# First block's attention: filler and output reads placed ahead of the row maxima, and the first query chunks rotated inside the third weight unit

## What is computed

```
for l in range(2):
    h = rmsnorm(x, g_pre_mix[l]);  z = h @ w_in[l]
    zf, zq, zk, zv, zm = split(z)            # Fourier, queries, keys, values, memory queries
    y_f = real(fft over tokens and channels of zf) @ w_f
    q, k = rope(zq), rope(zk)
    y_a = window attention(q, k, v)          # 8 query heads, 2 key heads, |i - j| <= 128, with a sink
    mkv = rmsnorm(mem) @ w_mem_kv[l]         # keys and values of 256 memory tokens
    y_m = memory attention(zm, mkv)          # 4 heads
    y = concat(rmsnorm of y_f, y_a, y_m) @ w_out[l]
    x = x + rmsnorm(y)
    x = x + rmsnorm(swiglu(rmsnorm(x)))
```

## Time and profile before

| | us |
|---|---|
| median of three runs | 3774.41 |
| lowest and highest | 3772.91 and 3779.49 |
| the profiled execution | 3766.36 |
| span of the core in that execution | 3764.6 |

### The profile page before, as it was taken

How to read it: one execution, slowest core, us unless ns; L and a number is a source line. 1 busy time by engine, 2 the same in 40 slices (tenths; PEclk the granted TensorE clock), 3 DMA queues, 4 the chain that set the end, 5 groups by cost and what they waited for, 6 DMA issues and landing times.

```text
span 3764.6 us, 49780 instructions
## 1 busy us (share of the span) xinstructions
PE 3558.8 (95%) x19681; PEld 2957.8 (79%) x19681; DVE 2481.9 (66%) x3545; ACT 1622.2 (43%) x2413; POOL 55.2 (1%) x82
## 2 busy tenths in 40 slices
PE   5899999889999999998899999999999989999999
PEld 4568997557998799886467889889988646778997
DVE  6548863656883688557665588649864766657862
ACT  3435542443553356325423345425542443234552
POOL 0000000000000000000000000000000000000000
PEclk8999999999999999999999999999999989999999
DMA  4212332212232233231123223223333211232332
GB/s 129 69 34 79 102 101 90 75 57 67 92 112 100 67 103 111 95 101 53 34 56 90 90 90 113 95 95 99 104 103 93 73 37 45 79 100 79 112 101 84
DMA packets 320877, 321.05 MB, mean 85 GB/s; under 512 B 11081, under 2 KB 292885, under 8 KB 320661
## 3 DMA queue, kind: packets, MB, share of 16 engines
q1 hardware_dynamic: 316308, 307.94, 25.9%
q0 software_dynamic: 2560, 8.26, 0.7%
q10 hardware_dynamic: 1792, 1.86, 0.2%
HBM read 315.92 MB, written 2.10 MB: 84 GB/s over the span
## 4 chain that ended last, share of the span: by engine, by line
PE 79%; DVE 15%; ACT 3%; issue 2%; DMA 0%; POOL 0%; ACTq 0%; DVEq 0%; POOLq 0%
PE products L733 31%; PE products L872 23%; PE products L770 6%; PE small L770 6%; PE small L872 4%; PE products L1066 2%; DVE conv L2588 2%; DVE w_lo L1877 1%; DVE seven_x L2110 1%; ACT w_hi L1330 1%; PE small L931 1%; DVE X L1892 1%; DVE x_sums L2099 1%; PE products L950 1%; PE products L1088 1%
## 5 line engine op out<-in xcount | busy, mean ns | idle before, releaser
L1877 DVE TENSOR_TENSOR w_lo<-raw,w_hi 128x2048 fp32r<-128x2048 f32 x190 | 435.3, 2291 | 528.8 <-ACT w_hi L1330 528.5
L1330 ACT ACTIVATE w_hi<-raw 128x2048 fp32r<-128x2048 f32 x190 | 363.4, 1913 | 943.6 <-PE products L733 691.8
L733 PE MATMUL products<-a_hi,w_hi 128*128 128x512 f32 (+1 forms) x1296 | 532.1, 411 | 35.4 <-DVE a_lo L1932 10.9
L733 PE MATMUL products<-a_lo,w_hi 128*128 128x512 f32 (+1 forms) x1296 | 519.7, 401 | 0.0
L733 PE MATMUL products<-a_hi,w_lo 128*128 128x512 f32 (+1 forms) x1296 | 519.5, 401 | 0.0
L872 PE MATMUL products<-seven_x,w_hi 128*128 128x256 f32 x2592 | 469.3, 281 | 7.7 <-DVE w_lo L2139 3.8
L872 PEld LDWEIGHTS products<-seven_x,w_hi 128*128 128x128 f32 x2592 | 398.0, 189 | 11.2 <-DVE w_lo L2139 5.1
L872 PE MATMUL products<-seven_x,more_hi 128*128 128x256 f32 x1632 | 381.7, 283 | 1.7 <-ACT rs_b L1421 1.7
L872 PE MATMUL products<-seven_x,w_lo 128*128 128x256 f32 x1296 | 363.1, 280 | 0.0
L733 PEld LDWEIGHTS products<-a_hi,w_hi 128*128 128x128 f32 (+1 forms) x1296 | 246.4, 190 | 109.4 <-issue 34.7
L733 PEld LDWEIGHTS products<-a_lo,w_hi 128*128 128x128 f32 (+1 forms) x1296 | 247.0, 191 | 63.7 <-issue 4.4
(11 more groups left out here) (421 smaller groups left out, 7372.4 us busy)
## 6 DMA issues: line engine op xcount, KB each, us to landing
raw<-in_ffn_w SPq DMA_DIRECT2D x244, 512.0 KB, 4.3
raw<-in_w_in SPq DMA_DIRECT2D x108, 512.0 KB, 4.8
raw<-in_w_ffn_in SPq DMA_DIRECT2D x88, 512.0 KB, 4.4
raw<-in_w_ffn_out SPq DMA_DIRECT2D x40, 512.0 KB, 4.4
raw<-in_w_out SPq DMA_DIRECT2D x32, 512.0 KB, 4.3
raw<-in_ffn_w SPq DMA_DIRECT2D x24, 384.0 KB, 3.5
raw<-in_w_mem_kv SPq DMA_DIRECT2D x8, 512.0 KB, 4.1
dft<-in_dft POOLq DMA_DIRECT2D x2, 2048.0 KB, 8.5
```

What stands on the lines that cost most here:

```text
L733: mm = pe.matmul(G[pair][0:m, into + b, 0:n], w[:, s, at:at + m], x, start=(first or into > 0) and k == 0 and q == 0, stop=(last or ends) ...
L1330: act.activation(w_hi[:, s, :], raw[:, s, :], ACT.Copy).then_inc(hi_ready, 1)
L1877: dve.tensor_tensor(w_lo[:, s, :], raw[:, s, :], w_hi[:, s, :].bitcast(F32), ALU.subtract).then_inc(lo_ready, 1)
```

## The change

Two orders are changed, both inside the first block's mixer.

First, query chunks 0 and 1 are rotated (`rotated_queries(0)`) at the end of the hook `during_queries`, into the pair `G` that the third unit does not use, and VectorE finishes them ahead of reading the third unit's result. `B4` and `B5` are no longer used for queries. Behind the third unit TensorE waits until its result is read, then rotates chunks 2 and 3 into the same spare pair. VectorE copies `B7` to `rs_b` ahead of making the low half of the fourth unit, and a new semaphore `spread_read` tells TensorE that `B7` is free.

Second, in the loop VectorE reads most fillers and all outputs of quad i-2 ahead of the maxima of quad i. Fillers 4 and 6 keep their place behind the maxima, since they are written in the same step.

```
                     mm.then_inc(four_ready, 1)
+                    rotated_queries(0)
+                spare = 1 - c.group % 2
+                def rotated_queries(first):
+                    pe.wait_ge(read_out[spare], c.next(f"read_out{spare}"))
+                    for i in range(2):
+                        pe.matmul(G[spare][:, i, :], c1["rot_q"][:], qT[:, first + i, :],
+                                  start=True, stop=True).then_inc(rot_ready, 1)
...
                 spread(MEM)
-                evicted((c.group - 2) % 2)
-                for i in range(2):
-                    pe.wait_ge(rot_used, c.next("rot_used"))
-                    pe.matmul((B4, B5)[i][:], c1["rot_q"][:], qT[:, i, :], start=True, stop=True).then_inc(rot_ready, 1)
-                pair = c.group % 2
-                pe.wait_ge(read_out[pair], c.next(f"read_out{pair}"))
-                evicted(1 - pair)
-                for i in range(2, 4):
-                    pe.matmul(G[pair][:, i - 2, :], c1["rot_q"][:], qT[:, i, :], start=True, stop=True).then_inc(rot_ready, 1)
+                evicted(1 - spare)
+                rotated_queries(2)
+                pe.wait_ge(four_copied, c.now("four_copied") + 1)
+                pe.wait_ge(spread_read, c.next("spread_read"))
+                pe.wait_ge(rot_used, c.next("rot_used", 2))
```

```
                 last.then_inc(diag_ready, 1)
+                late = 1 - c.group % 2
+                queries((G[late][:, 0, :], G[late][:, 1, :]), 0, late)
                 piece()
                 scaled(qT[:, 2:4, :], group(), rs)
+                dve.wait_ge(sum_ready, c.next("sum_ready"))
+                dve.tensor_copy(rs_b[:, 0:MEM], B7[:, 0:MEM]).then_inc(spread_read, 1)
+                dve.wait_ge(spread_read, c.next("spread_read"))
                 split_lo()
-                dve.wait_ge(sum_ready, c.next("sum_ready"))
-                stepped(dve.tensor_copy(rs_b[:, 0:MEM], B7[:, 0:MEM]))
-                settled()
-                queries((B4[:], B5[:]), 0)
-                late = group()
...
                         if i >= 2:
                             dve.wait_ge(t_ready, c.next("t_ready", quads[i - 2]["n"] // P))
+                        for n_fill in {1: (0,), 2: (1,), 3: (2,), 4: (3,), 5: (5,), 6: (7,)}.get(i, ()):
+                            fill_evict(n_fill)
+                        if i >= 2:
+                            out_evict(i - 2)
                         for r in (0, 2, 1, 3):
...
-                    if i >= 2:
+                    if i >= len(quads):
                         out_evict(i - 2)
-                    for n_fill in {1: (0,), 2: (1,), 3: (2,), 4: (3, 4), 5: (5, 6), 6: (7,)}.get(i, ()):
+                    for n_fill in {4: (4,), 5: (6,)}.get(i, ()):
                         fill_evict(n_fill)
```

## The result

| | before | after |
|---|---|---|
| median of four runs, us | 3773.66 | 3728.84 |
| lowest and highest | 3767.31 to 3779.49 | 3721.65 to 3741.45 |
| the profiled execution (its span) | 3766.36 (3764.6) | 3741.45 (3739.7) |

The ratio is 0.9885, with a 95% interval of 0.9867 to 0.9902: 43 us less (37 to 50). The profiled execution after is the slowest of its four, and that of before is faster than all of its four, so the two traces alone would show only 25 us. Before it lasts 144.1 and 146.3 us, after 128.2 and 128.2.

The account below looks back on a forecast made before the run. It took TensorE's waits for VectorE as the winnable bound: 6.9 + 3.0 + 19.9 + 1.6 + 4.2 = 35.6, less 1.5 for one clock slowdown, gives 34 us; 3774.4 - 34 = 3740.4 us. Range: 3730 to 3753.

Parts of the forecast that it names:

- the case over 40: Whole kernel: a gain of more than 40 us, chance 0.02.
- The head: Ahead of the first scores: moving two rotations starts them 3.44 us earlier per execution, 6.9 in all.
- The half clock behind the head: First scores behind the 4.72 us wait: their half clock goes, 1.5 us per execution, 3.0 in all.
- The fillers: Attention loop: all twelve TensorE waits for VectorE's reads of fillers go, 19.9 us over both executions.
- Step 7: Loop step 7: output read ahead of maxima gains 1.6 us per execution, plus 1.1 of half clock in the second; 4.2.
- The clock's terms: Half clock: 3.0 behind the head, 1.6 at a slow filler, 1.1 in step 7, less 1.5 for one slowdown.
- Rival (a): TensorE's remaining gaps: half clock comes more often, gain only 24 to 29 us, 3745 to 3750; chance 0.13.
- Rival (b): Loop: the chain from scores over maxima, exponentials and scaling to transposes becomes the bound; gain 22, 3752; chance 0.08.
- Rival (c): Loop: waits follow the fillers' own ends, so only the head gains, under 7.5 us, 3767 to 3774; chance 0.03.
- Rival (d): Attention: TensorE, without waits, drops its clock for long; slower, over 3782 us; chance 0.02.
- The thin cover: Head: VectorE's low half of weights ends only 0.3 us before the first filler wants it; TensorE pays any excess.
- the term of 1.6 us: Second execution: a filler slowed (4.57 against 2.98 us) behind a 2.0 us wait returns to full clock, 1.6 us.

Follow-up runs that it names:

- e1: The kernel before with only the head's change (query chunks 0 and 1 rotated earlier), loop order as before: 3752.35 us, ratio 0.9959.
- e3: The changed kernel timed and traced again with no edit: 3727.84 us, ratio 0.9889 to the kernel before.
- e11: The changed kernel, unedited, one more trace: 126.0 and 126.1 us for the two executions of the first block's attention.
- e4: The kernel before timed and traced again with no edit: 3772.14 us, ratio 1.0002.
- e10: The kernel before, unedited, one more trace: 146.2 and 146.1 us for the two executions of the first block's attention.
- e9: The kernel before with five useless matmuls in TensorE's 4.72 us wait ahead of the first scores: 3763.57 us, ratio 0.9981.
- e7: The changed kernel with four memsets on VectorE delaying the low half of weights made at the head: 3737.20 us, ratio 0.9910.
- e2: The kernel before with only the loop's reads moved ahead of the maxima, head as before: 3742.86 us, ratio 0.9925.
- e5: The changed kernel with outputs read behind the maxima again, fillers still ahead: 3736.48 us, ratio 0.9908 to the kernel before.

## Why the prediction was right, and where it was not

It said 3740.4 us by a gain of 34; the gain is 43 (37 to 50), in the direction forecast. The gain lies in the range as it was worded, a gain of 44 to 21, and the median of 3728.84 is 1.2 us below its low end of 3730. But a gain of 43 is not the forecast of 29 to 40, which had 0.72; it is the case over 40, which had 0.02. By the sections the gain is 39.2, inside the forecast, in part by luck, as the last point on the sum shows. Point by point:

- **The head, 3.44 us for each execution.** From the read of the chunks to the scores it was 94.39 - 75.00 = 19.39 us and is 92.22 - 76.11 = 16.11: 3.3. The wait left is 1.24, predicted 1.4. Right, within 0.2.
- **The half clock behind the head, 1.5.** From the first scores to the second it was 8.34 and is 99.09 - 92.22 = 6.87, at 1.00: 1.5. Right.
- **The fillers, twelve waits, 19.9.** All went. From the scores of step 1 to those of step 7 it was 169.69 - 102.73 = 66.96 us and is 154.83 - 99.09 = 55.74: 11.2 for each execution where the waits add up to 9.95. The other 1.3 are 0.2 at each of six waits: a filler that waited began after the tail of the transposes, one that doesn't begins within it (at 101.43, when the transposes last from 100.58 to 101.67). A wait in a row is less than what its removal gives. The two rows of before that this and the next point start from:

```profile
102.73 1.56 PE L1135 MATMUL small<-kT,qT 64*128 64x384 f32 x8
...
169.69 1.13 PE L1135 MATMUL small<-kT,qT 64*128 64x256 f32 x8
```

- **Step 7.** To the next scores it was 180.59 - 169.69 = 10.90 us and is 164.22 - 154.83 = 9.39: 1.5, predicted 1.6, with the two waits foretold (1.44 and 1.67 for 1.3 and 1.6). But the reason was not the order, and this step of the sum was wrong: the waits add up to 3.1 against 3.2, and with the old order at the full clock it is 9.27 (`e1`). The 1.5 are the half clock of the earlier trace rows, which the sum had counted only as 1.1 in the second execution. In the profile after the clock fell one wait later and took them back; in `e3` and `e11` it didn't.
- **The clock's terms: what was mis-sized.** By the sections the gain is 39.2, against 34. Without falls the sections differ by 2 x (140.4 - 126.0) = 28.8: some 6.6 at the head, 22.4 at the fillers and -0.3 in step 7, where the sum had 6.9, 19.9 and 3.2. The overlap at the fillers and the nothing of step 7 nearly cancel, and that is luck. What is left, 39.2 - 28.8 = 10.4, is the clock, where I had 3.0 + 1.6 + 1.1 - 1.5 = 4.2. There were eight falls on average before, and two thirds of one after. I had read them off the one execution that I had, as if they stood at fixed places. It had six; `e4` and `e10` had ten and eight. And I put a price only on places where this trace showed one.
- **Rival (a), more falls, 0.13.** The opposite happened: `e9` and `e1` show that falls behind the fillers' waits don't come from those waits alone. They were seen only in the kernel before, which has the head's 4.7 us of idle time too, and this change removes both. But `e7` has a fall behind a wait of 1.97 in step 1 with the short head, so the long wait isn't needed for one.
- **Rival (b), the chain over the exponentials.** No wait of that kind in steps 1 to 6 after; TensorE waits 9.4 us for scaled probabilities (8.9 before), in step 9 and behind step 11. `e7` shows how near it is: VectorE 2.4 us later at the head makes it 13.4.
- **Rival (c), waits that only move.** Wrong, as `e2` shows: the loop alone gives 28 us. **Rival (d), a long half clock.** Wrong: in the profile after the clock is 1.00 from the first scores to the second wait of step 7, 71 us on end. One window of it, with TensorE busy throughout:

```profile
108.00:124.00 16.00, 16.00 (x91) 11.05 (x92) 10.01 (x31) 8.53 (x21) 0.00 (x0) 1.00 0.18 60
```

- **The thin cover.** A wrong statement of the prediction, without harm to its number: I said of the head's low half that the first filler wants it. `e7` shows that it doesn't; step 2 does.

On the clock the prediction set a rule of the Trainium skill against the earlier trace rows: "TensorE: Matmul & The Clock Gate", section "Loop structure matters more than you think", says that VectorE's copy out of PSUM does not bring the clock down. The page says it of a loop in which the next matmuls follow immediately. Where that is so here, the trace agrees: in the profile after VectorE reads every filler with no wait of TensorE for it, and the clock stays at 1.00 from the first scores to step 7. In the row TensorE stood idle for 1.96 us until the read was done, and it is behind such idle time that the clock fell: at 0.66 in `e10`, at 0.55 behind a wait of 3.2 us in `e5`. It doesn't always: behind the same waits for fillers it is 1.00 in `e1` and `e9`. So the page's sentence doesn't bear on this term; the row does, and the term of 1.6 us was one of several such.

What stays open: which of the waits has a fall in a given execution, how the head's wait bears on those at the fillers, and why the falls outside of the sections differ between traces of one kernel (3472.0 to 3483.2 us there, after).

## What to carry to other kernels

When TensorE's waits are short and many, read the clock in more than one execution before pricing it. A fall of 1.5 us behind a wait of 1.4 doubles its cost, it comes and goes from execution to execution, and here the falls 25 us behind a long wait went with that wait. One wait of 3.2 us split into two of about half its size gained here although their sum stayed the same. Compare like sections of the traces and, within them, like stages: whole spans differ by things that the change did not touch. In a busy engine's list, put first what the engine that bounds the time waits for, and leave for later what has slack. What has slack is read from who waits for its result, not from where it stands in the code.

## What the runs showed of the hardware

- Behind the head's wait of 4.72 us the clock was at 0.50 for about 3 us. Five useless products in that wait keep it at 1.00 (`e9`). Then none of the twelve waits of 1.4 to 2.0 us for fillers is followed by a fall, where all three traces of before have one or two (at 732; at 120 and 741; at 119 and 737). `e1` agrees: no fall behind the same twelve waits. What in it does this, the idle time or the shift by 1.5 us, no run shows.
- A short wait can be followed by half clock with no long one ahead in the section: 1.97 us in `e7` (fall from 104 on), 1.67 us in the profile after, 1.5 us in `e9` and `e7` (fall from 80 on). Waits of these sizes are followed by 1.00 elsewhere (1.44 us in the profile after, 1.96 in `e1`).
- At the sections' ends the clock stays at 0.50 for 10 to 17 us in every trace. How long changes from execution to execution, and nothing was tried on it.
- The same kernel's sections differ by 126.0 to 128.2 us (after) and 144.1 to 148.7 (before) between executions: by falls of 1.5 to 1.9 us each (2.7 for two in a row), and by 0.6 where the stretch at the end is the longer one.
- A group of matmuls that follows without a wait starts 0.06 to 0.25 us ahead of where the record of the one before ends. The ends of matmul records are modelled by the profile, so this tells of starts.
